# Order of a pair of experts in the mixture-of-experts stage of a two-layer trunk

## The reference, cut to what matters

```
a = jnp.einsum('bld,edf->blef', h, w1)
b = jnp.einsum('bld,edf->blef', h, w3)
act = jax.nn.silu(a) * b * gate[..., None]
moe = jnp.einsum('blef,efd->bld', act, w2)
x = x + g2 * moe
```

## Time and profile before

| | |
|---|---|
| median of three runs | 1331.83 us |
| profiled execution, its own time | 1331.29 us |
| its span | 1329.5 us |
| PE busy | 1246.7 us (94%) |
| DVE, ACT, POOL busy | 367.2, 226.8, 13.0 us |
| read from HBM | 354.53 MB, a mean of 269 GB/s |
| expert pieces, 1 MB each | 204, median 10.9 us from issue to landing |
| `moe_in` (line 857) | 2048 matmuls, 225.0 us busy |
| `moe_out` (line 893) | 512 matmuls, 113.4 us busy |

### The profile page before, as it was taken

One profiled execution on the slowest core, in us unless ns is written; L12 is line 12 of the kernel. 1 busy time (PEld: TensorE's weight loads), 2 busy tenths in 40 slices (PEclk: granted clock), 3 DMA queues, 4 the chain that ended last, 5 costly groups with the idle time before them and its releaser, 6 DMA issues.

```text
span 1329.5 us, 18353 instructions
## 1 busy us (share of the span) xinstructions
PE 1246.7 (94%) x7708; PEld 940.5 (71%) x7708; DVE 367.2 (28%) x910; ACT 226.8 (17%) x439; POOL 13.0 (1%) x28
## 2 busy tenths in 40 slices
PE   3999999999999999999969999999999799999994
PEld 2588888788877666666547888887887676666652
DVE  1431153223235111111242223423233511111113
ACT  2241012321031100111024101223101110000111
POOL 1000000000000000000000000000000000000000
PEclk9999999999988999999979999999999699999998
DMA  9886333324676999999937933333344399999990
GB/s 383 324 347 254 130 140 135 127 100 164 243 276 282 420 418 420 420 421 419 413 142 259 365 137 128 118 135 119 127 159 146 157 420 420 420 421 421 420 402 34
DMA packets 49964, 358.47 MB, mean 270 GB/s; under 512 B 5664, under 2 KB 5680, under 8 KB 7120
## 3 DMA queue, kind: packets, MB, share of 16 engines
q1 hardware_dynamic: 47808, 348.15, 65.8%
q0 software_dynamic: 2064, 9.03, 1.8%
HBM read 354.53 MB, written 2.62 MB: 269 GB/s over the span
## 4 chain that ended last, share of the span: by engine, by line
PE 88%; DVE 4%; DMA 4%; ACT 2%; issue 2%; POOL 0%; DVEq 0%; SPq 0%; ACTq 0%; POOLq 0%
PE bank L626 28%; PE bank L857 15%; PE bank L893 9%; PE bank L767 6%; PE bank L840 5%; PE bank L786 4%; PE bank L934 4%; PE bank L618 3%; PE bank L553 3%; DMA ring<-in_experts 2%; DMA par<-in_params 2%; PE bank L872 1%; PE bank L606 1%; ACT gates L1353 1%; PE bank L798 1%
## 5 line engine op out<-in xcount | busy, mean ns | idle before, releaser
L626 PE MATMUL bank<-h,ring 128*128 128x256 f32 x1664 | 375.2, 384 | 4.3 <-ACT h L1126 4.0
L626 PEld LDWEIGHTS bank<-h,ring 128*128 128x128 f32 x1664 | 316.2, 192 | 56.9 <-issue 12.4
L857 PE MATMUL bank<-ring,gates 128*64 128x256 f32 x2048 | 225.0, 380 | 4.4 <-ACT gates L1353 3.7
L857 PEld LDWEIGHTS bank<-ring,gates 128*64 128x64 f32 x2048 | 150.2, 137 | 76.9 <-issue 5.7
L893 PE MATMUL bank<-ring,gates 128*64 128x512 f32 x512 | 113.4, 594 | 5.4 <-ACTq L1356 5.4
L893 PEld LDWEIGHTS bank<-ring,gates 128*64 128x64 f32 x512 | 41.5, 137 | 66.9 <-issue 66.9
L840 PE MATMUL bank<-uc,gates 128*128 128x128 f32 x576 | 71.2, 285 | 0.0
L840 PEld LDWEIGHTS bank<-uc,gates 128*128 128x128 f32 x576 | 69.9, 202 | 0.0
L1444 DVE SCALAR_TENSOR_TENSOR gates<-gates,bank 128x512 f32<-128x512 f32 (+1 forms) x18 | 11.8, 658 | 181.8 <-issue 135.6
L934 PEld LDWEIGHTS bank<-gates,uc 128*128 128x128 f32 x256 | 47.3, 190 | 18.8 <-issue 13.0
L934 PE MATMUL bank<-gates,uc 128*128 128x256 f32 x256 | 59.5, 386 | 0.0
(11 more groups left out here) (232 smaller groups left out, 1020.8 us busy)
## 6 DMA issues: line engine op xcount, KB each, us to landing
ring<-in_experts SPq DMA_DIRECT2D x204, 1024.0 KB, 10.9
ring<-in_weights SPq DMA_DIRECT2D x128, 1024.0 KB, 4.9
cst<-in_consts POOLq DMA_DIRECT2D x1, 1537.0 KB, 16.0
par<-in_params POOLq DMA_DIRECT2D x2, 749.5 KB, 12.6
x<-in_x_in POOLq DMA_DIRECT2D x1, 1024.0 KB, 10.4
sc<-in_s_cache POOLq DMA_DIRECT2D x2, 512.0 KB, 9.3
y_out<-h POOLq DMA_DIRECT2D x2, 512.0 KB, 3.0
kc<-in_k_cache POOLq DMA_DIRECT2D x2, 256.0 KB, 6.0
```

Of the source, the lines that this page charges most:

```text
L626: last = pe.matmul(bank[b][:, c * TOK:(c + 1) * TOK], w[:, k, c * P:(c + 1) * P], h[:, k, :], start=(k == 0), stop=(k == KT - 1))
L857: last = pe.matmul(bank[b][64 * j:64 * j + 64, half * 256:half * 256 + 256], hgat[:, k, 64 * j:64 * j + 64], w[j][:, k, :], start=(k == 0) ...
```

## The change

In the loop over pairs, PE's order becomes `moe_in(p)`, `moe_out(p-1)` with its combine, `act_turn(p)`, `gather(p+1)`. ACT's and DVE's orders are changed to match. SP's order of the pieces, the semaphores and their counts, the banks and all shapes are the same.

```diff
@@ PE
                     moe_in(layer, p)
-                    gather(layer, p + 1)
-                    act_turn(layer, p)
                     if p:
                         moe_out(layer, p - 1)
+                    act_turn(layer, p)
+                    gather(layer, p + 1)
                     if layer + 1 < DEPTH and p >= 4:
                         filter_step(layer + 1, p - 4)
@@ ACT, behind the tanh of pair p
-                    if p + 1 < ITEMS:
-                        gathered(p + 1)
+                    if 0 < p < PAIRS:
+                        out_low(p - 1)
                     sc_e.wait_ge(s_act_turned, n + 1)
                     sc_e.activation(flat(actT[p % 2])[:, 0:wide], bank[6][:, 0:wide],
                                     ACT.Copy).then_inc(s_actT_ready, 1)
                     sc_e.wait_ge(s_actT_ready, n + 1)
                     sc_e.sem_inc(s_bank_free[6], 1)
-                    if p:
+                    if p + 1 < ITEMS:
+                        gathered(p + 1)
+                    else:
                         out_low(p - 1)
@@ DVE, behind the second multiply of pair p
                     dve.sem_inc(s_bank_free[7], 1)
+                    if p:
+                        out_high(p - 1)
                     if p + 1 < ITEMS:
                         gathered(p + 1)
-                    if p:
-                        out_high(p - 1)
```

## The result

The changed kernel took 1342.8 us in the median of its first four runs, against 1330.56 for the kernel before in four: ratio 1.0085, 95% interval 1.0062 to 1.0108. Twelve more runs, against 35 of the kernel before on the same chip, gave 1340.85 against 1332.19 us, ratio 1.0060, interval 1.0039 to 1.0080. So it is 8 to 12 us slower; I had forecast 6.3 us. The second, larger comparison is the better measure: +8.7 us.

The account below looks back on a forecast made before the run. The expert stages were taken as bound by the weight stream, 29.89 us a pair against PE's 29.47. Late moe_out pieces add 3.0 and 3.3 us to 1331.29, giving 1337.6 profiled and a forecast of 1338.1 us, range 1332 to 1343.

Parts of the forecast that it names:

- What bounds the kernel: Expert stages: the weight stream needs 29.89 us a pair, PE 29.47, so the second layer is at the edge of both.
- PE's terms: PE's steps in a pair: +0.44 us for act_turn, -0.24 for fewer tiling changes, -0.10 for a shorter wait; 29.57 us.
- The first pair's +0.4 us: Start of each layer's stage: act_turn(0) waits for DVE's second multiply, so moe_in(1) starts 0.4 us later.
- The copy is paid once there too. Cost of all these: none: Filter steps: they wait for bank 4 behind the gather and moe_in follows at once, so no added cost.
- The ring: Moe_out's last pieces are wanted 17.3 us into a pair, not 22.3, so PE waits for them: +6.3 us.
- 1 us of delay is covered: Weight stream: 2.1 us of queue ahead of a piece absorbs moe_in's slots being freed about 1 us later, without gaps.
- each layer's term: Time added to each layer's expert stage by late moe_out pieces: +3.3 us in the first, +3.0 in the second.
- the filter steps give the stream room: First layer behind pair 4: PE sets the pace from there, 91.3 us for the following periods and steps.
- there is more room: Later in a layer: pieces take 11 to 13 us to land, so later slot releases are covered.
- the stream keeps up: Expert stages: moe_out's pieces land earlier and are never late, only PE's small costs remain; +1.1 us, 1332.9 us, chance 0.18.
- The ring runs empty: Expert stages: late releases leave DMA idle 1 us a pair, +14 us over 14 pairs, about 1350 us; chance 0.05.
- the likeliest case: Whole kernel: the main forecast of 1338.1 us, +6.3 us from late moe_out pieces, 1336 to 1341 us, chance 0.58.

Follow-up runs that it names:

- the light kernels: Expert transfers cut to 1536 of 2048 columns, in the kernel before and in the changed one: medians 1332.68 and 1333.41 us, against 1332.19 for the kernel before.

## Why the prediction was right, and what it missed

- *What bounds the kernel*: right. PE's pair is just under the stream's, and with lighter transfers the order hardly matters.
- *PE's terms*: right, to 0.03 us each. The period without late pieces is 29.47 us, 0.10 under my sum: moe_out takes 6.97 behind moe_in, not 7.02, and the gather with its copy a few hundredths less. The first pair's +0.4 us came out as 0.38. "The copy is paid once there too. Cost of all these: none" for the filter steps was wrong by 0.6 us, in the first layer alone.
- *The ring*: right as a mechanism, with waits of 0.3 to 1.4 us a pair from pair 1 on where I had "0.3 us or so". The stage of the second layer hangs on the last moe_out piece, as I placed it: 1278.9 + 0.1 + 12.2 = 1291.2.
- *The step that failed* is "1 us of delay is covered", the claim that the stream runs on without loss. I took 6.8 - 4.7 = 2.1 us of queue as cover. But what counts in the table above is the margin to the first of sixteen landing events, and the stream loses from some 2 us down. The piece that I read, issued at 1107.3, has a margin of 2.5 us: 0.5 us of delay is covered, not 1. In the new order a margin falls under 2 us in 2 to 7 of the pairs of each layer. So each layer's term was too small: 4.5 and 4.4 us over three traces where I had 3.3 and 3.0. In the second layer the last piece lands 1.2 us later, and 1.3 to 1.8 us are lost at such margins; of the first layer's 1.2 us, half is the filter steps.
- In the first layer I held that "the filter steps give the stream room" behind pair 4, and that later in the layer "there is more room". In pair 7 moe_in frees slots so late that the stream is short itself; the window of the pair, and two us of it:

```profile
617.83:649.51 31.68, 30.86 (x219) 19.50 (x218) 5.09 (x13) 3.83 (x6) 0.00 (x0) 1.00 0.98 402
...
622.00:624.00 2.00, 2.00 (x22) 1.35 (x20) 0.00 (x0) 0.00 (x0) 0.00 (x0) 1.00 0.72 221
```

  The piece issued at 621.5 lands 4.8 us later, as one alone does. The waits in that pair are 0.2 us even so. The first layer's waits lie ahead of it: in three traces moe_out is 3.9, 2.9 and 4.5 us longer than without late pieces, 2.9, 2.3 and 4.2 of this up to pair 4, where I had 2.2.
- *Rivals*: "the stream keeps up" came true only in the light kernels. "The ring runs empty" I put at 5 in 100, as 1 us of idle DMA a pair. With eight slots it happened in that size only in pair 7 of the first layer; its mild form, 0.1 to 0.9 us in some pairs, is the missing 2.4 us but for the 0.6 of the filter steps, as far as the traces tell, and I should have put part of it into the forecast itself.
- *The time*: the median of the first four runs, 1342.8 us, lies 0.2 us inside the upper end of the range and above the 1336 to 1341 of the likeliest case; that it lies inside is in part luck. The twelve later runs, 1340.85, are the firmer number.

What stays open: the landing events fit sixteen DMA engines that are not in step, the first of which has no work while the queue still holds pieces for the others. No run changed the spread of the engines by itself, and why it differs from piece to piece (1.2 us in one place, 3.3 in another) is not known.

## What to carry to other kernels

Where a weight ring and TensorE run at nearly one pace, an order is judged by when in the loop each piece is wanted and when its slot is freed, not by what TensorE does: here the order cost TensorE 1.4 us, and waiting for the stream 7.5. Spread the steps that use weights over the loop, and put those that use none between them. Before a reorder, compute for the last piece of each round its landing less its wanted time, and hold the issue of each piece against the landing of the piece ahead: a queue that isn't empty is not yet cover. When a change moves the first release of a stage, count that delay once for the whole stream.

## What was not expected of the hardware

The stream loses time before its queue is empty. At a margin over 2 us (a piece's issue to the first of sixteen landing events of the piece ahead) 1801 pieces of 1 MB lost 0.02 us each, at 1.5 to 2 us 42 pieces lost 0.25, and at 0 to 1 us 13 pieces lost 0.82. A mean rate over a stage doesn't show this, since it holds the stand at the start too: full pairs move 417 to 421 GB/s in the old order, and 419 or 420 in five of the second layer's seven in the new order, with 408 and 407 in the two others.
